# Linear-attention stage of a hybrid block: low-rank rows loaded whole at unit 7, forget-row sums behind unit 1, eight gate tiles ahead of eight split tiles

## The reference, cut to what matters

```python
h = rmsnorm(x, norm_g)
proj = h @ w_in
(g_q, g_k, g_v, g_lr, g_gate, f_q, f_k, f_v, f_fg, f_gate,
 m_q, m_gate) = jnp.split(proj, idx, axis=-1)
z_alpha = g_lr @ w_alpha_up + b_alpha                  # g_lr: 16 columns, the low-rank rows
log_a = jax.nn.log_sigmoid(z_alpha) / GLA_GATE_NORM    # decay of linear attention
o_gla = rmsnorm(gla_chunked(g_q, g_k, g_v, log_a), gla_norm_g) * jax.nn.silu(g_gate)
log_f = jax.nn.log_sigmoid(f_fg + b_forget)            # 6 columns, the forget rows
o_fox = fox_attention(f_q, f_k, f_v, log_f) * jax.nn.silu(f_gate)   # uses cumsum(log_f)
o_mem = memory_attention(m_q, mk, mv) * jax.nn.silu(m_gate)
return rmsnorm(x + concatenate([o_gla, o_fox, o_mem]) @ w_out, final_norm_g)
```

## Time and profile before

| what | us |
|---|---|
| median of 3 runs | 1448.46 (1448.29 to 1450.61) |
| the profiled execution, own time | 1449.48 |
| its span, first to last instruction | 1447.7 |
| TensorE matmul busy | 1295.8 |
| vector, scalar, POOL busy | 670.4, 546.8, 415.2 |
| mean granted TensorE clock | 0.949 of full |

### The profile page before, as it was taken

How to read it: one execution, slowest core, us unless ns; L and a number is a source line. 1 busy time by engine, 2 the same in 40 slices (tenths; PEclk the granted TensorE clock), 3 DMA queues, 4 the chain that set the end, 5 groups by cost and what they waited for, 6 DMA issues and landing times. The chain is left out here.

```text
span 1447.7 us, 20370 instructions
## 1 busy us (share of the span) xinstructions
PE 1295.8 (90%) x6624; PEld 1044.4 (72%) x6624; DVE 670.4 (46%) x1622; ACT 546.8 (38%) x1131; POOL 415.2 (29%) x464
## 2 busy tenths in 40 slices
PE   5898798799999999999988495999999999599997
PEld 4887565588877777778866363777777678478886
DVE  4563313210145445440008374887888888432222
ACT  3563102301222222221117383777777777410010
POOL 5223420002234444541102584224322322300000
PEclk9999898799999999999998697999999999799999
DMA  6453221122344544442118455141632611355453
GB/s 215 141 161 110 61 66 50 64 78 78 104 149 144 160 146 148 160 126 77 61 49 220 143 115 128 46 140 28 153 93 61 162 23 23 113 205 212 177 188 131
DMA packets 118447, 170.40 MB, mean 118 GB/s; under 512 B 11957, under 2 KB 74677, under 8 KB 116517
## 3 DMA queue, kind: packets, MB, share of 16 engines
q1 hardware_dynamic: 115864, 160.65, 36.9%
q10 hardware_dynamic: 2304, 8.39, 1.4%
q0 software_dynamic: 192, 0.33, 0.2%
HBM read 103.19 MB, written 66.13 MB: 117 GB/s over the span
## 5 line engine op out<-in xcount | busy, mean ns | idle before, releaser
L836 PE MATMUL cg_cps<-h_T,tok_slot 128*128 128x512 f32 x2112 | 502.6, 398 | 10.7 <-DVE cg_stage L1030 10.7
L836 PEld LDWEIGHTS cg_cps<-h_T,tok_slot 128*128 128x128 f32 x2112 | 403.1, 192 | 101.8 <-DVE cg_stage L1030 11.1
L1718 PE MATMUL out_yps<-out_w,out_mix 128*128 128x512 f32 x768 | 177.0, 393 | 19.8 <-DMA out_mix<-scr_mix 17.3
L1718 PEld LDWEIGHTS out_yps<-out_w,out_mix 128*128 128x128 f32 x768 | 145.4, 190 | 51.2 <-DMA out_mix<-scr_mix 17.5
L1558 DVE TENSOR_SCALAR_CACHE_REDUCE fox_prob<-fox_sps 128x512 f32<-128x512 f32 (+2 forms) x240 | 142.0, 607 | 36.3 <-PE fox_sps L1443 33.4
L1520 ACT ACTIVATE fox_pT<-fox_tps 128x512 fp32r<-128x512 f32 x240 | 124.4, 530 | 88.8 <-PE fox_tps L1453 86.2
L1569 DVE TENSOR_TENSOR fox_pT<-fox_tps,fox_pT 128x512 fp32r<-128x512 f32 x240 | 141.7, 605 | 21.6 <-ACT fox_pT L1520 20.9
L1453 PE MATMUL fox_tps<-all_ident,fox_prob 128*128 128x128 f32 x816 | 134.7, 278 | 15.3 <-ACT fox_prob L1512 8.4
L1466 PE MATMUL fox_ops<-fox_pT,fox_v 128*128 128x512 f32 x480 | 137.3, 376 | 0.0
L1453 PEld LDWEIGHTS fox_tps<-all_ident,fox_prob 128*128 128x128 f32 x816 | 99.9, 141 | 45.4 <-ACT fox_prob L1512 11.8
L1438 PE MATMUL fox_sps<-fox_ka,fox_qa 128*128 128x512 f32 (+2 forms) x240 | 106.5, 444 | 17.2 <-PEq L1375 13.7
(11 more groups left out here) (187 smaller groups left out, 1681.2 us busy)
## 6 DMA issues: line engine op xcount, KB each, us to landing
scr_split<-cg_stage SPq DMA_DIRECT2D x64, 256.0 KB, 2.8
out_mix<-scr_mix SPq DMA_DIRECT2D x32, 512.0 KB, 4.2
tok_xin<-in_w_cols SPq DMA_DIRECT2D x22, 512.0 KB, 4.4
tok_xin<-in_x SPq DMA_DIRECT2D x16, 512.0 KB, 3.8
scr_gates<-cg_stage SPq DMA_DIRECT2D x32, 256.0 KB, 2.4
out_x<-in_x SPq DMA_DIRECT2D x16, 512.0 KB, 6.2
out<-out_o ACTq DMA_DIRECT2D x16, 512.0 KB, 5.0
scr_fox_v<-tok_vst SPq DMA_DIRECT2D x16, 384.0 KB, 3.0
```

What stands on the lines that cost most here:

```text
L836: mm = nc.tensor.matmul(cps[u % 2][:, :], w[j % 2][a_][:, kk, :], hT[b_][:, kk, c * CH:(c + 1) * CH], start=(kk == 0 and r == 0), stop=(kk ...
L1718: mm = nc.tensor.matmul(yps[s][:, c, :], mix[s][a][:, kk, :], w[b][:, kk, c * CH:(c + 1) * CH], start=(kk == 0 and n == 0), stop=(kk == MI ...
```

## The change

Three edits in one stage, and the list of tiles on the host.

- The 16 low-rank rows are loaded whole (16 x 2048) by one DMA at unit 7 of SP's loop, with one semaphore and one buffer in place of two; SP's wait for `rows_stored` moves from unit 10 to unit 7, its waits for the logits go, and TensorE waits for the load once, at unit 10.
- The vector engine's last three instructions of the forget rows move into its unit loop, ahead of the copy of unit 2. The bias stays where it is; so does all of the scalar engine's and POOL's work on these rows.
- All eight gate tiles come before the eight split tiles: units 24 to 55 are gates and 56 to 87 split. The numbers of the gates and of the split tiles in scratch memory stay.

```diff
--- before.py
+++ after.py
@@ -519,15 +519,15 @@
 class ColumnUnits:
 
 
-    KINDS = ["raw"] * NRAW + ["gate"] * 3 + ["split"] * NSPLIT + ["gate"] * (NGATE - 3)
-    FIRST_SPLIT = NRAW + 3
+    KINDS = ["raw"] * NRAW + ["gate"] * NGATE + ["split"] * NSPLIT
+    FIRST_SPLIT = NRAW + NGATE
     UNITS = NCOL * NCH
     G0 = 36
     STEPS = T // P
 
     @classmethod
     def gate_index(cls, j):
-        return j - NRAW if j < cls.FIRST_SPLIT else j - cls.FIRST_SPLIT - NSPLIT + 3
+        return j - NRAW
 
     @classmethod
     def sends(cls, u):
@@ -560,7 +560,7 @@
     PAIRS = 2
     QKW = GLA_H * GLA_DK
     Z_UNITS = {10 + 2 * g: g for g in range(NCH)}
-    CLEAR_UNIT = 24
+    LR_UNIT, CLEAR_UNIT = 7, 24
     gs = 1.0 / GLA_GATE
     ctx = ExitStack()
     with ctx:
@@ -587,7 +587,7 @@
         decay_ctx = ExitStack()
         with decay_ctx:
             kz = Pools(nc, decay_ctx, "decay")
-            lr = [kz.sb(f"lr{s}", [GLA_R, CH]) for s in range(2)]
+            lr = kz.sb("lr", [GLA_R, T])
             keep, zabs, la, bz = (kz.sb(n, [KR, PAIRS, CH]) for n in ("keep", "zabs", "la", "b"))
 
         q, kk_, b = ([k.sb(f"{n}{s}", [KR, PAIRS, P]) for s in range(2)] for n in ("q", "k", "b"))
@@ -608,9 +608,9 @@
          dve_rows, pool_rows, rows_stored) = map(
             k.sem, ("w_hi w_lo projected hi_done evacuated stored0 stored1 bias_loaded rows_t rows_copied act_rows "
                     "dve_rows pool_rows rows_stored").split())
-        (pads, w_loaded, gn_loaded, lr_loaded0, lr_loaded1, kept, z_done, z_abs, z_min, z_exp, z_ln, la_done, b_done,
+        (pads, w_loaded, gn_loaded, lr_loaded, kept, z_done, z_abs, z_min, z_exp, z_ln, la_done, b_done,
          b_stored, cleared) = map(
-            k.sem, ("pads w_loaded gn_loaded lr_loaded0 lr_loaded1 kept z_done z_abs z_min z_exp z_ln la_done b_done "
+            k.sem, ("pads w_loaded gn_loaded lr_loaded kept z_done z_abs z_min z_exp z_ln la_done b_done "
                     "b_stored cleared").split())
         (in_loaded0, in_loaded1, v_loaded0, v_loaded1, gate_loaded0, gate_loaded1, tail_done, ep_done, em_done, ee_done, vT_done, v_copied,
          qd_done, qpad_done, k_decayed, prep_done, kT_done, attn_done, kv_done, o_done, oT_done, k_copied, masked,
@@ -620,7 +620,7 @@
                     "qd_done qpad_done k_decayed prep_done kT_done attn_done kv_done o_done oT_done k_copied masked "
                     "state_done squared ms_done rstd_done on_done gate_ready mixed mix_hi mix_lo mix_stored0 "
                     "mix_stored1").split())
-        cols_loaded, stored, lr_loaded = tk.cols_loaded, (stored0, stored1), (lr_loaded0, lr_loaded1)
+        cols_loaded, stored = tk.cols_loaded, (stored0, stored1)
         in_loaded, v_loaded, gate_loaded = (in_loaded0, in_loaded1), (v_loaded0, v_loaded1), (gate_loaded0, gate_loaded1)
         mix_stored = (mix_stored0, mix_stored1)
         IN_DMAS = 16 * 5
@@ -700,13 +700,11 @@
                     if c == 0 and j + 2 < NCOL:
                         sp.wait_ge(w_lo, j + 1)
                         sp.dma_start(w_raw[j % 2][:, :, :], w_cols[j + 2]).then_inc(cols_loaded[j % 2], 16)
+                    if u == LR_UNIT:
+                        sp.wait_ge(rows_stored, 80)
+                        sp.dma_start(lr[:, :], scr.lr).then_inc(lr_loaded, 16)
                     if u in Z_UNITS:
                         g = Z_UNITS[u]
-                        if g == 0:
-                            sp.wait_ge(rows_stored, 80)
-                        if g >= 2:
-                            sp.wait_ge(z_done, PAIRS * (g - 1))
-                        sp.dma_start(lr[g % 2][:, :], scr.lr[:, g * CH:(g + 1) * CH]).then_inc(lr_loaded[g % 2], 16)
                         if g >= 1:
                             sp.wait_ge(b_done, g)
                             sp.dma_start(scr.gla_b[:, :, (g - 1) * CH:g * CH], bz[:, :, :]).then_inc(b_stored, 16)
@@ -733,13 +731,13 @@
             @block.tensor
             def _(pe):
                 def decay_logits(g):
-                    pe.wait_ge(lr_loaded[g % 2], 16 * (g // 2 + 1))
                     if g == 0:
+                        pe.wait_ge(lr_loaded, 16)
                         pe.wait_ge(w_loaded, 16 * 8)
                     else:
                         pe.wait_ge(z_min, PAIRS * g)
                     for p in range(PAIRS):
-                        nc.tensor.matmul(kvps[p][0:KR, :], wup[p][:, :], lr[g % 2][:, :], start=True, stop=True
+                        nc.tensor.matmul(kvps[p][0:KR, :], wup[p][:, :], lr[:, g * CH:(g + 1) * CH], start=True, stop=True
                                          ).then_inc(z_done, 1)
 
                 def key_side(n):
@@ -1029,17 +1027,20 @@
                             dve.wait_ge(stored[s], CU.sent_before(u))
                         nc.vector.tensor_copy(stage[s][HI][:, :], cps[s][:, :]).then_inc(evacuated, 1)
 
+                def forget_sums():
+                    dve.wait_ge(act_rows, 3)
+                    nc.vector.scalar_tensor_tensor(f, f, 0.0, a, ALU.min, ALU.subtract).then_inc(dve_rows, 1)
+                    dve.wait_ge(dve_rows, 2)
+                    nc.vector.memset(a, -3e38).then_inc(dve_rows, 1)
+                    dve.wait_ge(dve_rows, 3)
+                    nc.vector.tensor_tensor_scan(f, f, a, 0.0, ALU.add, ALU.max).then_inc(dve_rows, 1)
+
                 dve.wait_ge(rows_copied, 1)
                 dve.wait_ge(bias_loaded, 16)
                 nc.vector.tensor_scalar(f, f, bf[:, 0:1], None, ALU.add).then_inc(dve_rows, 1)
-                dve.wait_ge(dve_rows, 1)
-                dve.wait_ge(act_rows, 3)
-                nc.vector.scalar_tensor_tensor(f, f, 0.0, a, ALU.min, ALU.subtract).then_inc(dve_rows, 1)
-                dve.wait_ge(dve_rows, 2)
-                nc.vector.memset(a, -3e38).then_inc(dve_rows, 1)
-                dve.wait_ge(dve_rows, 3)
-                nc.vector.tensor_tensor_scan(f, f, a, 0.0, ALU.add, ALU.max).then_inc(dve_rows, 1)
                 for u in range(CU.UNITS):
+                    if u == 2:
+                        forget_sums()
                     if u in Z_UNITS:
                         log_decays(Z_UNITS[u])
                     n, half_step = CU.step_at(u)
@@ -1814,8 +1815,8 @@
         "w_out", "final_norm_g")}
     w = np.ascontiguousarray(inputs["w_in"])[0].reshape(KT, P, -1)
     starts = ([G_Q + P * i for i in range(6)] + [G_GATE + P * i for i in range(3)]
-              + [F_Q + P * i for i in range(3)] + [M_Q + P * i for i in range(2)] + [F_K + P * i for i in range(3)]
-              + [F_GATE + P * i for i in range(3)] + [M_GATE + P * i for i in range(2)])
+              + [F_GATE + P * i for i in range(3)] + [M_GATE + P * i for i in range(2)]
+              + [F_Q + P * i for i in range(3)] + [M_Q + P * i for i in range(2)] + [F_K + P * i for i in range(3)])
     a["w_cols"] = np.ascontiguousarray(np.stack([w[:, :, c:c + P].transpose(1, 0, 2) for c in starts]))
     tok = np.concatenate([w[:, :, F_V:F_V + 384], w[:, :, F_FG:F_FG + FOX_H], w[:, :, G_LR:G_LR + GLA_R]], axis=2)
     a["w_tok"] = np.ascontiguousarray(tok.transpose(1, 0, 2))
```

## The result

| | before | after |
|---|---|---|
| median of 4 runs | 1448.58 (1448.29 to 1450.61) | 1409.93 (1408.84 to 1411.04) |
| profiled execution, span | 1447.7 | 1409.3 |
| mean granted TensorE clock | 0.949 | 0.962 |
| scalar engine busy | 546.8 | 571.5 |

A forecast was written before the change was run, and what follows sets the result against it. TensorE bounds the column projection, with two faults: idle behind unit 1 and waits on the low-rank load, both doubled by the clock. 13.7 - 6.8 + 34.7 - 1.5 = 40.1 us gained, giving 1408.4, range 1402 to 1427.

The forecast's parts named there:

- Forget-row sums, 13.7: Behind unit 1: moving the sums removes 10.69 us of TensorE idle and 3.01 of low clock afterwards, 13.7 gained.
- Unit 8, 6.8 lost: At unit 8: TensorE newly waits 3.8 us for POOL's split of tile 2, plus 3.0 of low clock; 3.8 to 8.7.
- clock term: Behind the new idle at unit 8: a lowered clock costs 3.0 us, from a possible 0 to 4.9.
- long hole: Behind units 0 and 1 in the kernel before: 10.69 us of TensorE idle, whose low clock then cost 3.0.
- Low-rank rows, 34.7: From the end of unit 9 to that of unit 17: 34.7 us gained, 17.6 waiting and 17.1 clock.
- The order, 1.5 lost: All gates before splits: table switches cost nothing; a split unit at the stage's end costs 1.5 us (1.2 to 2.5).
- slack of 2.96: In a linear-attention step: exponentials end at 574.80, the vector engine takes them at 577.76, covering a table load of 1.28.
- Rival B: At the logit blocks: the clock falls anyway, so only 17.6 us of waiting is gained there; 1425.5, 17 in 100.
- Rival D: Ten steps turned to gates: late exponentials, 2.2 us idle plus 2.3 clock each, 45 lost; 1453.4, 3 in 100.
- 6 us at 0.50 behind unit 8: Sign of being right: behind a hole of about 4 us until POOL's split near 189, some 6 us at clock 0.50.

The follow-up runs named there:

- early split: The changed kernel with POOL's split of tile 2 placed ahead of its first wait for the forget rows' stores; 1405.26 us, ratio 0.9695.
- gate tile at the end: The changed kernel with the eighth gate tile left as the last tile of all, behind the split tiles; 1410.16 us.
- blocks of four: The changed kernel with each logit matmul issued four times into the same place, at units 10, 12, 14 and 16; 1449.06 us, once.
- K = 2: The changed kernel with two pairs of tiny Exp and Silu activations ahead of each linear-attention step's exponentials; 1432.88 us, once.
- K = 3: The changed kernel with three pairs of tiny Exp and Silu activations ahead of each linear-attention step's exponentials; 1511.09 us, once.

## Why the prediction was right, step by step

- *Forget-row sums, 13.7*. The two copies run as their units end and unit 4 doesn't wait. From the first matmul to the end of unit 9 the gain is 7.9; with the new hole's 5.3 added back that is 13.2. The missing 0.5 is not the change's: behind the idle time ahead of the stage the granted clock was 0.50 until about 144.0 in the changed kernel, 1.6 us into unit 0, and until about 141.7 before, 0.7 into it.
- *Unit 8, 6.8 lost*. The mechanism, the place and the releaser are as forecast; the size was 5.3: 3.41 of idle and 12.80 for two units, 16.21 where the full clock needs 10.88. Idle is near the 3.8 of the forecast. The clock is 1.6 (12.80 against the 11.18 of the same 48 matmuls at 1.00), not 3.0; the 0.3 left over is the modelled end of a row's last matmul, which counts as busy but which no next matmul waits for. The clock term was mis-sized by taking it from the long hole. Its fall came later: after unit 8 had begun at 190.39 the clock was still 1.00, and then below for about 3.4 us:

```profile
190.40:191.40 1.00, 1.00 (x4) 0.85 (x5) 0.00 (x0) 0.00 (x0) 0.95 (x1) 1.00 0.08 25
...
192.40:193.40 1.00, 1.00 (x4) 0.81 (x3) 0.00 (x0) 0.00 (x0) 1.00 (x1) 0.50 0.58 234
...
195.40:196.40 1.00, 1.00 (x6) 0.82 (x5) 0.00 (x0) 0.00 (x0) 0.00 (x0) 1.00 0.00 0
```

  It need not have fallen at all, as three of the nine profiles with such a hole show, so its place in the sum is in part luck. The early split shows the whole worth of this hole, 5.1.
- *Low-rank rows, 34.7*. 33.0 measured. The 1.7 less can be read from the rows: a logit block lasts 1.89 from its start to the next matmul, not 1.7 (start to start, 203.12 to 205.01), and the two units behind it 11.11, not 10.88 (205.01 to 216.12). Four times 0.19 and 0.23 make the 1.7. SP's earlier wait cost nothing: the load went out at 185.71, the store of unit 7 at 187.73, its copy having begun at 187.01.
- *The order, 1.5 lost*. 1.4 measured at the end, shown in the profiles of the order alone and of the gate tile at the end. In the medians it is not proved: with the order they are 0.9, 1.4 and 1.9 higher than without it in three pairs, each within the spread, and the gate tile at the end made it no lower. The forecast that the table switches cost nothing in the ten steps holds; TensorE is busy in every one of the 140 us of this row:

```profile
360.00:500.00 140.00, 140.00 (x746) 1.00 0.38 118
```

  How they are covered stands in one step of the changed kernel:

```profile
471.12 1.28 ACT L858 ACT_TABLE_LOAD   x1
...
472.42 0.42 ACT L858 ACTIVATE cg_em<-cg_b 112x256 f32<-112x256 f32 x1
...
473.05 0.40 ACT L861 ACTIVATE cg_ep<-cg_b 112x256 f32<-112x256 f32 x1
473.47 1.28 ACT L898 ACT_TABLE_LOAD   x1
...
474.60 0.42 DVE L961 SCALAR_TENSOR_TENSOR cg_qd<-cg_q,cg_ep 112x256 f32<-112x256 f32 x1
```

  The exponentials end at 473.45 and are taken at 474.60: of the slack of 2.96, 1.15 is left. The activation follows the load by 0.02 us. Behind the vector engine, POOL takes them at 476.44 and TensorE's key side starts at 479.59; with more loads in front, the table above found the end of the cover some 4.8 us later. The Trainium skill (ScalarE: Activation LUTs, What ACT_TABLE_LOAD costs) gives about 1.38 us of drain beside the load; these rows show none, and the measurement decides.
- *Rival B* was wrong for this kernel, right as a mechanism. The blocks of 1.9 us leave the clock at 1.00, so in the kernel before it took the waits to lower it. But the idea behind my argument, that light work with no idle time leaves the clock up, is refuted by the blocks of four. Whether the light blocks had a share in the falls before is open. The Trainium skill's remark that transposes don't count as ordinary matmuls do for the clock (TensorE: Matmul & The Clock Gate, Part 4: PE-mode transpose) speaks of another instruction; the blocks of four hold ordinary matmuls, and no run here tests transposes alone.
- *Rival D* was put at 4.5 us per step from 2.2 of idle. No run has just that wait. With 1.2 of idle a step cost 1.4 and no clock, with 2.8 it cost 4.6, so the price is of the right kind but the clock's share does not set in with the first idle time. The kernel ends slower than before only somewhere between K = 2 and K = 3.
- *The sum*: 40.1 forecast, 39.5 in the stage, 38.4 in the span and 38.7 in the medians. What lies between is outside the stage. That the sum is within 0.6 of the stage is partly luck: the loss at unit 8 was forecast 1.5 too large and the gain of the low-rank rows 1.7 too large, and the two cancel. The profile didn't have the 6 us at 0.50 behind unit 8 that I had named as a sign; it had 3.4.

## What to carry to other kernels

A small load that TensorE waited for in the middle of dense work cost its wait nearly twice here: 17.6 us of waiting were 33 us of time, since the clock went down with it and the matmuls behind paid. Waits of 1.2 us did not do this, so read the clock beside each wait. When such a hole is filled, ask which engine's work was hidden behind it: here POOL's split came up next, and moving it into POOL's own wait for its stores gave another 5 us. Placing work by kind, as with the gates, brought nothing here, where the engines that it relieves have slack, and in the profiles it cost 1.4 us by what then stood last before a barrier.

## What the runs showed of the hardware that I had not expected

- Light matmuls (16 rows of contraction) were followed by a fall of the granted clock from 1.00 to 0.50 with TensorE busy all the time, in blocks that would last 7.6 us at full clock; blocks of 1.9 us were not (one run with four such blocks).
- A hole of 3.3 to 3.6 us before full work was followed by a lowered clock in six profiles and not in three others, the same program included (12.77 and 11.18 us for the same two units), and the fall came after the work had begun again.
